# Turning and scaling rows in one product: what a diagonal operand does to the entrances of a two-layer backbone

## The reference

```
for l in range(2):
    ul = rmsnorm(hl, norm_g[l, 0]) * (1.0 + sc1) + sh1        # first entrance
    uc = rmsnorm(hc, norm_g[l, 0]) * (1.0 + csc1) + csh1
    mc, ml = token_mixer(uc, ul, ...)                         # DeltaNet, retention, attention, Fourier, gates
    hl = hl + g1 * rmsnorm(ml, norm_g[l, 1])
    vl = rmsnorm(hl, norm_g[l, 2]) * (1.0 + sc2) + sh2        # second entrance
    hl = hl + g2 * rmsnorm(ffn(vl), norm_g[l, 3])             # l = 0: SwiGLU, l = 1: top-2 of 8 experts
    # the context stream hc goes the same way in layer 0 only
rmsnorm(x, g) = x * rsqrt(mean(x * x, axis=-1) + 1e-6) * g
```

## Time and profile before

| what | us |
|---|---|
| median of 3 runs (lowest, highest) | 2141.61 (2135.06, 2147.99) |
| the profiled execution | 2141.93 |
| its span | 2140.1 |
| PE busy in the span | 2069.6 |
| DVE busy in the span | 1568.6 |
| ACT busy in the span | 1150.5 |

### The profile page before, as it was taken

How to read it: one execution, slowest core, us unless ns; L and a number is a source line. 1 busy time by engine, 2 the same in 40 slices (tenths; PEclk the granted TensorE clock), 3 DMA queues, 4 the chain that set the end, 5 groups by cost and what they waited for, 6 DMA issues and landing times. The chain is left out here.

```text
span 2140.1 us, 35983 instructions
## 1 busy us (share of the span) xinstructions
PE 2069.6 (97%) x14738; PEld 1717.7 (80%) x14738; DVE 1568.6 (73%) x2201; ACT 1150.5 (54%) x1581; POOL 143.3 (7%) x118
## 2 busy tenths in 40 slices
PE   8999899999999999998998999999999999999997
PEld 5887787888888888876776899788888888888886
DVE  4546665889567555447466667699999999999998
ACT  4253433332432222234544345588888888888886
POOL 0013520000000000000045100100000000000000
PEclk9999999999999999999999999999999999999999
DMA  6700034454154545413000544599999999999995
GB/s 265 272 18 1 3 121 157 177 207 170 76 222 187 207 182 194 175 62 114 25 2 3 218 178 158 205 392 383 375 386 381 383 375 386 382 371 390 377 411 197
DMA packets 68485, 470.11 MB, mean 220 GB/s; under 512 B 7712, under 2 KB 8672, under 8 KB 14048
## 3 DMA queue, kind: packets, MB, share of 16 engines
q1 hardware_dynamic: 62464, 441.62, 53.2%
q10 hardware_dynamic: 4704, 21.98, 2.6%
q0 software_dynamic: 1152, 4.19, 0.5%
HBM read 455.15 MB, written 12.62 MB: 219 GB/s over the span
## 5 line engine op out<-in xcount | busy, mean ns | idle before, releaser
L2439 DVE TENSOR_TENSOR wsp_l<-ring,wsp_h 128x1024 fp32r<-128x1024 f32 x528 | 643.2, 1223 | 46.9 <-ACT wsp_h L1549 12.1
L1549 ACT CAST wsp_h<-ring 128x1024 fp32r<-128x1024 f32 x528 | 555.3, 1054 | 135.0 <-PE bank L718 79.1
L716 PE MATMUL bank<-wsp_h,xTs_h 128*128 128x512 f32 x704 | 282.5, 401 | 1.0 <-issue 0.6
L718 PE MATMUL bank<-wsp_h,xTs_l 128*128 128x512 f32 x704 | 275.4, 391 | 0.0
L717 PE MATMUL bank<-wsp_l,xTs_h 128*128 128x512 f32 x704 | 274.1, 389 | 0.0
L2069 ACT CAST dsp_h<-ring 128x1024 fp32r<-128x1024 f32 x66 | 69.2, 1048 | 244.3 <-PE bank L1424 172.7
L3036 DVE TENSOR_TENSOR dsp_l<-ring,dsp_h 128x1024 fp32r<-128x1024 f32 x66 | 80.9, 1225 | 145.5 <-ACT dsp_h L2069 145.2
L1317 PE MATMUL bank<-u_hi,gsp_h 128*128 128x512 f32 (+1 forms) x512 | 174.1, 340 | 0.0
L1317 PE MATMUL bank<-u_hi,gsp_l 128*128 128x512 f32 (+1 forms) x512 | 172.1, 336 | 0.0
L1317 PE MATMUL bank<-x_lo,gsp_h 128*128 128x512 f32 (+1 forms) x512 | 172.0, 336 | 0.0
L2345 DVE SCALAR_TENSOR_TENSOR products<-ring,cond_rows 128x1024 bf16<-128x1024 f32 x128 | 156.4, 1222 | 5.0 <-DVE dsp_l L3036 0.5
(11 more groups left out here) (399 smaller groups left out, 4104.3 us busy)
## 6 DMA issues: line engine op xcount, KB each, us to landing
ring<-in_moe_tiles_dram SPq DMA_DIRECT2D x264, 1024.0 KB, 7.0
ring<-in_ada_tiles_dram SPq DMA_DIRECT2D x48, 1024.0 KB, 4.8
ring<-in_ffn_tiles_dram SPq DMA_DIRECT2D x33, 1024.0 KB, 6.8
ring<-in_gate_tiles_dram SPq DMA_DIRECT2D x32, 1024.0 KB, 6.8
ring<-in_in_tiles_dram SPq DMA_DIRECT2D x22, 1024.0 KB, 6.0
arena<-in_branch_tiles_dram ACTq DMA_DIRECT2D x8, 1024.0 KB, 7.6
ring<-in_out_tiles_dram SPq DMA_DIRECT2D x8, 1024.0 KB, 4.7
x_rows<-arena SPq DMA_DIRECT2D x1, 3584.0 KB, 16.0
```

Source lines behind the costliest of these rows:

```text
L716: pe.matmul(o, xTs[0][:, kk, :], whi[:, k, :], start=(kk == 0), stop=False)
L718: mm = pe.matmul(o, xTs[1][:, kk, :], whi[:, k, :], start=False, stop=(kk == KD - 1))
L1549: act.copy(wsp[0][:, g % 4, :], half_slot(MOE0, g)).then_inc(s.gq_o.up, 1)
L2439: v.tensor_tensor(wsp[1][:, g % 4, :], half_slot(MOE0, g), wsp[0][:, g % 4, :], ALU.subtract).then_inc(s.gq_pt.up, 1)
```

## The change

The factor of each row is no longer multiplied into the row. DVE multiplies the identity by the factors instead, which gives a diagonal of 128 x 128 in the first 128 words of the tile's place in `xs2` or `xs_next`. PE then forms, for each piece, the product of the unscaled piece of `h` (stationary) with the diagonal (moving): `h_piece.T @ diag(x)`, the turned and scaled piece. Before, the scaled piece was the stationary operand and the identity the moving one, in PE's transpose mode. Semaphores, banks and their order stay as they are.

```diff
@@ next_T (PE, first entrance of layer 1)
                         for k, c in part_rows(0, g, b):
-                            mm = transpose(bank[part_banks(0, g) + b][:, c.start + P * i:c.start + P * (i + 1)],
-                                           xs_next[:, t, P * k:P * (k + 1)])
+                            mm = pe.matmul(bank[part_banks(0, g) + b][:, c.start + P * i:c.start + P * (i + 1)],
+                                           h[:, t, P * k:P * (k + 1)], xs_next[:, t, 0:P], start=True, stop=True)
@@ normalised_T (PE, second entrances)
-                                mm = transpose(bank[part_banks(l, g) + b][:, c.start + P * i:c.start + P * (i + 1)],
-                                               xs2[:, t, P * k:P * (k + 1)])
+                                mm = pe.matmul(bank[part_banks(l, g) + b][:, c.start + P * i:c.start + P * (i + 1)],
+                                               h[:, t, P * k:P * (k + 1)], xs2[:, t, 0:P], start=True, stop=True)
@@ next_norm (DVE)
-                v.tensor_scalar(xs_next[:, t, :], h[:, t, :], x, None, ALU.mult).then_inc(above.xs1.up, 1)
+                v.tensor_scalar(xs_next[:, t, 0:P], ident, x, None, ALU.mult).then_inc(above.xs1.up, 1)
@@ norm_tile (DVE)
-                    v.tensor_scalar(xs2[:, t, :], h[:, t, :], x, None, ALU.mult).then_inc(s.xs2.up, 1)
+                    v.tensor_scalar(xs2[:, t, 0:P], ident, x, None, ALU.mult).then_inc(s.xs2.up, 1)
```

## The result

The changed kernel takes 2146.47 us (median of 20 runs, 2140.46 to 2151.0), the kernel before, run beside it, 2142.15 (20 runs, 2135.06 to 2147.99). The ratio is 1.0017, 95% interval 1.001 to 1.0025: slower by about 4 us, within the 0.5% that was named as no change, and inside the forecast range. The profiled execution took 2148.34 with a span of 2146.5, 6.4 more than that of before; it lies 1.9 above its own median, so it overstates the difference.

A forecast was written before the change was run, and what follows sets the result against it. PE was taken as the bound, busy 2069.6 of 2140.1 us. Layer 0 +3.2, layer 1's entrances -1.2 and +1.55 make 3.5 us onto 2141.93: 2145.4, stated as 2145, range 2138 to 2152.

The forecast's parts named there:

- Price of a turned piece: On PE at all turns: a product is two records, 0.223 us against 0.109; 80 products add 9.1 us.
- The second rival: All turns: a full fp32 product costs PE four transposes, 0.437 us; sum 15.8, time 2157.7; chance 0.05.
- Price of a scaling: Ten DVE scalings shrink from 0.753 to 0.281 us, 0.47 less each, gained where DVE is waited for.
- Layer 0: Second entrance of layer 0, two turns: the feed-forward starts 3.2 us later; the weight split stays hidden.
- Entrance of layer 1: First entrance of layer 1, where PE waits on DVE and ACT: shorter scalings bring -1.2 us at full clock.
- The clock there: First entrance of layer 1: PE busy twice as long likely keeps the granted clock at 2.4 GHz, about 3 to 2.
- The sum for the lower level: First entrance of layer 1 with the clock fallen to 1.2 GHz: +0.65 us in place of -1.2.
- Router passage: Second entrance of layer 1: +1.55 us for both turns; at tile 3 DVE is early and PE's fillers late.
- What passes on: Feed-forward and expert stages: PE has no slack, so delays pass on whole; own lengths change at most a microsecond or two.
- The sum: Whole kernel: 3.2 - 1.2 + 1.55 = 3.5 us added; forecast 2145, chance 0.52.
- Products for nothing: Third rival, all turns: the exchange costs PE nothing; -2.0 us, time 2139.9; chance 0.06.
- The fallen clock: First rival, first entrance of layer 1: the clock falls as before; sum +5.4, time 2147; chance 0.33.

The follow-up runs named there:

- The halves: Two kernels, each with one half of the edit against the kernel before: products with rows scaled in full (1.003), small scalings with transposes (0.9991).
- twice: Kernel before with each piece turned twice by a transpose, the second over the first, rows scaled in full; 2148.5 us, ratio 1.0037.
- after_3rd: The changed kernel run a third time with no edit of its own, against the kernel before; 2145.54 us, ratio 1.0025.
- full_scaling: Kernel before with ordinary fp32 products by the identity in place of transposes, rows still scaled in full on DVE; 2148.66 us, ratio 1.003.
- small_scaling: DVE scales only the identity, PE transposes the unscaled rows, row factors left out of the result; 2139.03 us, ratio 0.9991 against before.

## Why the prediction was right, step by step

- **Price of a turned piece.** Said: two records, 0.1116 apart, from the gather's products. Measured: 160 records, 0.1115 apart. The Trainium skill's "TensorE: Matmul & The Clock Gate", section Terms, has the transpose mode four times faster for FP32. The measurement decides against it here: twice. The second rival was built on that price. Its working has a slip on which nothing rests: by its own terms a product of 0.33 us gives a sum of about 8.7 us, and 10 is passed at about 0.35.
- **Price of a scaling.** Said 0.281 from rows with the same types, measured 0.287: 0.466 less each in place of 0.472.
- **Layer 0.** Said +3.2, measured +3.18. Each intermediate number is met: the fillers end at 598.39 (598.37), the turn starts at 598.49 (598.46), the weight split ends at 590.97 (591.1) and stays hidden. The halves show the exchange: +3.65 for the products, -0.47 for the one scaling that was waited for.
- **Entrance of layer 1.** Said -1.2, measured -1.31. With the 3.30 taken off, tile 2's scaling ends at 962.98 (963.0) and tile 3's at 964.43 (964.45). ACT was the limit behind them, as said: it ran without a wait, starting this bank 0.12 earlier than worked out (968.95 less 3.30 is 965.65, not 965.77), and DVE's split and PE's product followed it.
- **The clock there.** Said 3 to 2 for the higher level. Of seven executions with products in this entrance six kept it, of seven with transposes none did. So the outcome was right, but the reason was not: `twice` had the records and lost the clock. This part of the forecast came out by luck. The sum for the lower level was too high, 0.30 measured for 0.65. I had taken the lower level for the whole of both late tiles; in the execution that showed it, it began at 964.7, inside tile 2, and was over at 968.1, with 13 of PE's 32 records begun after that. On this the Trainium skill's "TensorE: Matmul & The Clock Gate", Part 4: PE-mode transpose, says that transposes don't count as activity in the way that other products do. The counts of six and none lean its way, but the rows of before and of `twice` have the clock rise after nothing but transposes, so as a flat rule it doesn't hold, and products didn't keep the clock for certain either (after_3rd). What sets the clock in this entrance stays open.
- **Router passage.** Said +1.55, measured +1.46. The turn starts 0.08 earlier than worked out (1364.59 less 4.74 is 1359.85, not 1359.93). The order of events is the one foreseen: DVE early, PE's fillers late.
- **What passes on.** The feed-forward changed its own length by 0.04, the experts theirs by 0.25 (in the two repeats of the changed kernel, against the first trace of before: -0.07 and +0.14). PE is still busy for all of the one and for 747.8 of 750 us of the other, as two windows of after show beside the earlier trace rows:

```profile
603.00:947.00 344.00, 344.00 (x1573) 287.08 (x1572) 185.66 (x254) 92.54 (x117) 0.00 (x0) 1.00 0.46 177
...
1381.00:2131.00 750.00, 747.76 (x3390) 612.63 (x3390) 703.56 (x722) 614.62 (x731) 8.05 (x7) 1.00 0.97 377
```

- **The sum.** Said +3.5, measured +3.33 in the touched stretches. The step that failed is one the working didn't have: it let everything between the entrance and the router pass unchanged. The mixer of layer 1 was 2.9 longer in the profiled execution, so the whole difference was 6.4. The medians of the three comparisons of the changed kernel with before differ by 4.3 (20 runs), 8.7 (5) and 4.9 (12), weighted by runs 5.1: some 1.8 above the touched stretches, with intervals of 1.6, 2.9 and 2.6 us to either side, which hardly tell it from nothing. The forecast of 2145 was missed by 1.5, of which 0.5 is the median of before itself, 2142.15 over 20 runs where the three shown ones gave 2141.61.
- **The rivals.** Products at four transposes: excluded by the spacing. Products for nothing: excluded, `full_scaling` has +5.56 against `small_scaling`'s -2.15. The fallen clock: real, in one of three executions of the changed kernel.

## What to carry to other kernels

Price an exchange of work between two engines at each place by who is waited for there: the same edit cost 3.2 and 1.5 us where PE ran without a break and DVE was hidden or nearly so, and brought 1.3 where PE waited for a chain of DVE and ACT. Do only the last (2138.3 us, ratio 0.9988, and 0.9987 when repeated). For a fp32 piece of 128x128, an ordinary product takes twice a transpose's time on PE, and a gain of under half a microsecond on the other engine has to pay for eight of these differences.

Instructions added ahead of a dense stage shift it in the instruction stream, and a stretch that no edit touches changed by 3 to 6 us with that. Untouched stages also wander by some microseconds with no change at all. Compare stages by the same instruction's start in both traces, and in more than one trace of each kernel, before putting a difference of the total down to the edit.

## What the runs showed of the hardware

- **Pauses at fixed counts of PE's instructions.** A pause of 0.5 to 1.8 us in a dense stream of small products moved when 128 idle instructions were put into the feed-forward ahead of it, and was back at 256. In all fourteen traces 143 of 155 pauses of this kind stand whole multiples of 256 instructions apart, give or take one. The Trainium skill, "Advanced Engine Details and Errata", section ISA Cache, gives a cache line of 16 KB, 256 instructions; the distance of 256 and the 16 KB of a packet agree. That the pause is the fetch of such a block is inferred from this; no row shows the engine waiting for it. The Trainium skill's "Runtime: NRT & Kernel Launch", section Instruction fetch mechanics, calls the cost of such a boundary mostly hidden. In the feed-forward (344.00 busy of 344.00, with 3144 instructions and so some twelve multiples of 256) it is; in the scan, where 59 records fit into 1.09 us, it wasn't always.
- **The scatter of the runs goes with the granted clock.** Over the 110 runs of before whose clock is listed, on four chips, the span rises by 0.35 us for each us at 1.2 GHz (correlation 0.89; 37 us at that level in a mean run).
- **A clock at half speed need not cost anything.** In `small_scaling`'s entrance the 16 transposes took 3.56 us in place of some 1.9, and the entrance was as short as that of the changed kernel with the full clock, 22.56 against 22.57. In five traces with the transposes and scalings of before the clock was down for 6.8 to 13.7 us around this entrance, and it took 23.88 to 23.90 in each. But in the changed kernel, with twice the records, the fall cost 1.6 us (24.18 against 22.57).
